# Prompt attention: VectorE's compressed step split around one copy, and the mask conversions placed in the compression stage

## What is computed

```python
s_c = jnp.einsum('bqghd,bngd->bghqn', qg, kc).astype(jnp.float32)
p_c = masked_softmax(s_c, m_c)
o_c = jnp.einsum('bghqn,bngd->bqghd', p_c.astype(vc.dtype), vc)
...
s_s = jnp.einsum('bqghd,bgqkd->bghqk', qg, ks).astype(jnp.float32)
p_s = masked_softmax(s_s, m_s)
o_s = jnp.einsum('bghqk,bgqkd->bqghd', p_s.astype(vs.dtype), vs)
...
s_w = jnp.einsum('bqghd,bkgd->bghqk', qg, k_win).astype(jnp.float32)
p_w = masked_softmax(s_w, m_w)
o_w = jnp.einsum('bghqk,bkgd->bqghd', p_w.astype(v_win.dtype), v_win)
...
o = g[..., 0:1] * o_c + g[..., 1:2] * o_s + g[..., 2:3] * o_w
```

## Time and profile before

| | |
|---|---|
| median of 3 runs | 4078.23 us (4076.43 to 4082.27) |
| the profiled execution | 4081.6 us, its span 4080.0 us, mean granted TensorE clock 0.973 |
| busy over the span | PE 93%, DVE 44%, ACT 23%, POOL 30% |
| prompt attention | from 2443.0 to 2991.3 us of the span |
| in 2500 to 2600 us | PE 93.11, DVE 60.67, ACT 58.77, POOL 60.18 us busy |

### The profile page before, as it was taken

One profiled execution on the slowest core, in us unless ns is written; L12 is line 12 of the kernel. 1 busy time (PEld: TensorE's weight loads), 2 busy tenths in 40 slices (PEclk: granted clock), 3 DMA queues, 4 the chain that ended last, 5 costly groups with the idle time before them and its releaser, 6 DMA issues. The chain is left out here.

```text
span 4080.0 us, 54787 instructions
## 1 busy us (share of the span) xinstructions
PE 3813.7 (93%) x20290; PEld 2936.2 (72%) x20290; DVE 1812.0 (44%) x3004; ACT 941.9 (23%) x2132; POOL 1215.9 (30%) x1021
## 2 busy tenths in 40 slices
PE   8999989998799999999999988999979999999999
PEld 5666666666576888878877766666657688888887
DVE  4565456654443111126662216666645411112766
ACT  3333332333210000000000005656531000000001
POOL 0211112111132333324341105656533233332432
PEclk9999999999699999999999999999989999999999
DMA  4010101100041111123331220000033111111322
GB/s 147 29 40 26 37 27 42 37 26 27 32 125 65 41 41 41 41 82 104 90 124 34 71 76 30 1 2 1 1 94 93 65 41 41 41 41 48 123 86 80
DMA packets 321874, 223.99 MB, mean 55 GB/s; under 512 B 28427, under 2 KB 313220, under 8 KB 319812
## 3 DMA queue, kind: packets, MB, share of 16 engines
q1 hardware_dynamic: 316020, 214.98, 17.7%
q0 software_dynamic: 2048, 5.25, 0.4%
q10 hardware_dynamic: 3650, 1.64, 0.2%
HBM read 191.54 MB, written 34.37 MB: 55 GB/s over the span
## 5 line engine op out<-in xcount | busy, mean ns | idle before, releaser
L773 PE MATMUL ps<-xT,work 128*128 128x272 f32 x2688 | 643.4, 392 | 0.0
L773 PEld LDWEIGHTS ps<-xT,work 128*128 128x128 f32 x2688 | 510.7, 190 | 105.3
L1269 PE MATMUL ps<-xn,work 128*128 128x363 f32 (+1 forms) x1536 | 548.6, 476 | 6.6 <-issue 6.5
L773 PE MATMUL ps<-xn,work 128*128 128x272 f32 x2016 | 489.9, 392 | 3.9 <-DVE work L844 3.9
L773 PEld LDWEIGHTS ps<-xn,work 128*128 128x128 f32 x2016 | 382.9, 190 | 83.9 <-issue 5.1
L387 PE MATMUL ps<-work 128*128 128x272 f32 x1676 | 402.4, 396 | 12.0 <-PEq L741 4.3
L387 PEld LDWEIGHTS ps<-work 128*128 128x128 f32 x1676 | 319.5, 191 | 83.5 <-issue 16.0
L2919 POOL TENSOR_SCALAR work<-work 128x640 f32<-128x640 f32 (+4 forms) x192 | 313.7, 1644 | 196.7 <-DVE work L2822 196.3
L1269 PEld LDWEIGHTS ps<-xn,work 128*128 128x128 f32 x1536 | 261.2, 192 | 102.8 <-issue 18.6
L646 POOL TENSOR_TENSOR xT<-xT,work 128x272 f32<-128x272 f32 x96 | 198.3, 2079 | 263.9 <-DVE work L512 167.1
L1963 POOL TENSOR_TENSOR xT<-xT,consts 128x512 f32<-128x512 f32 x96 | 133.6, 1405 | 453.7 <-DVEq L1793 386.2
(11 more groups left out here) (425 smaller groups left out, 5865.1 us busy)
## 6 DMA issues: line engine op xcount, KB each, us to landing
work<-in_ffn_w_in_dram SPq DMA_DIRECT2D x88, 512.0 KB, 4.9
xn<-in_ffn_w_out_dram SPq DMA_DIRECT2D x46, 704.0 KB, 4.5
work<-in_gdn_w_in_dram SPq DMA_DIRECT2D x32, 512.0 KB, 4.2
work<-in_ffn_w_out_dram SPq DMA_DIRECT2D x18, 704.0 KB, 4.5
ffn_parked_residual<-xT SPq DMA_DIRECT2D x2, 4352.0 KB, 12.8
work<-in_gdn_w_out_dram SPq DMA_DIRECT2D x32, 256.0 KB, 2.8
work<-in_nsa_w_out_dram SPq DMA_DIRECT2D x64, 128.0 KB, 2.9
xT<-ffn_parked_residual SPq DMA_DIRECT2D x4, 1632.0 KB, 10.2
```

The costliest lines, as they stand in the source:

```text
L773: ins = pe.matmul(acc(a, n), w[:, k, :], t[:, k, a * SUB:(a + 1) * SUB], start=(first and k == 0), stop=(k == HK - 1), skip_group_check=True)
L1269: mm = pe.matmul(unit_acc(u, m), w[j % 2][:, k, :], c.xn[:, k, o:o + cnt], start=(k == 0), stop=(k == KD - 1))
```

## The change

There are three edits. In `compress_stage` DVE now makes the bf16 masks and the memset between `keep_bias(0)` and `keep_pairs(1)`; the attention's own conversions, the semaphore and PE's wait for it are gone. `low_masks` only gives both stages the same addresses. In DVE's loop `maxima(k)` takes a list of groups. At the 7 c steps inside the list, g = 0 is done first, then `coefficients(k-1)` and `keep(k-3)`, and then g = 1. In the iteration behind a c step (where k - 1 is the c step), `keep(k-3)` comes before `coefficients(k-1)` and no longer after it.

```diff
@@ compress_stage, vector @@
                 keep_pairs(0)
                 keep_bias(0)
+                ident_low, causal_low, far_low, cmp_low = low_masks(a)
+                dve.tensor_copy(ident_low, const(c, "ident"))
+                dve.tensor_copy(causal_low, const(c, "causal_add"))
+                dve.tensor_copy(far_low, const(c, "far_add"))
+                for x in range(2):
+                    o, _ = CONST[f"cmp_add{4 * x}"]
+                    dve.tensor_copy(cmp_low[x], c.ct[:, o:o + 4 * NCMP])
+                dve.memset(a.rows[:, 0:NC, 4 * P:5 * P].rearrange("p i (g n) -> p i g n", g=2)[:, :, :, NCMP:DH], 0.0)
                 keep_pairs(1)
...
+def low_masks(a):
+
+    low = [a.rows[:, n, 2 * P:3 * P].bitcast(mybir.dt.bfloat16) for n in range(4)]
+    return low[0][:, 0:P], low[0][:, P:2 * P], low[1][:, 0:P], [low[2 + x][:, 0:4 * NCMP] for x in range(2)]
...
@@ prompt_attention, tensor @@
-                pe.wait_ge(low_ready, 1)
                 for k in range(NK + 4):
                     if k < NK:
                         scores(k)
@@ prompt_attention, vector @@
-                def maxima(k):
+                def maxima(k, gs):
                     t, kind, i = steps[k]
-                    for g in range(2):
+                    for g in gs:
                         dve.wait_ge(sc[g], k + 1)
...
-                dve.tensor_copy(ident_low, const(c, "ident"))
-                dve.tensor_copy(causal_low, const(c, "causal_add"))
-                dve.tensor_copy(far_low, const(c, "far_add"))
-                for x in range(2):
-                    o, _ = CONST[f"cmp_add{4 * x}"]
-                    dve.tensor_copy(cmp_low[x], c.ct[:, o:o + 4 * NCMP])
-                dve.memset(pc[:, :, :].rearrange("p i (g n) -> p i g n", g=2)[:, :, :, NCMP:DH], 0.0).then_inc(low_ready, 1)
+                def compressed(k):
+                    return 0 < k < NK and steps[k][1] == "c"
+
                 for k in range(NK + 3):
                     if k < NK:
-                        maxima(k)
+                        maxima(k, (0,) if compressed(k) else (0, 1))
+                    if compressed(k - 1):
+                        keep(k - 3)
                     if 1 <= k <= NK:
                         coefficients(k - 1)
-                    if 3 <= k:
+                    if 3 <= k and not compressed(k - 1):
                         keep(k - 3)
+                    if compressed(k):
+                        maxima(k, (1,))
```

More of the change, by code:

```diff
@@ L2572, in prompt_attention @@
     QT = TP // P
-    BF16 = mybir.dt.bfloat16
     steps = [(0, "c", None)]
@@ L2585, in prompt_attention @@
     pts = [dead[:, n * 512:(n + 1) * 512] for n in range(RING)]
-    low = [a.rows[:, n, 2 * P:3 * P].bitcast(BF16) for n in range(4)]
-    ident_low, causal_low, far_low = low[0][:, 0:P], low[0][:, P:2 * P], low[1][:, 0:P]
-    cmp_low = [low[2 + x][:, 0:4 * NCMP] for x in range(2)]
+    ident_low, causal_low, far_low, cmp_low = low_masks(a)
     probs = {"s": [[take(c, TP) for g in range(2)] for _ in range(2)], "w": [[take(c, 5 * P) for g in range(2)] for _ in range(2)]}
@@ L2658, in prompt_attention @@
     with ExitStack() as ctx:
-        low_ready, sc0, sc1, mx0, mx1, ex0, ex1, cst, cf, scaled, wscaled, tr, kv, ka, multiplied, od = sems(
-            nc, ctx, c, "masks_ready", "scores0_done", "scores1_done", "maxima0_ready", "maxima1_ready", "probs0_ready", "probs1_ready",
+        sc0, sc1, mx0, mx1, ex0, ex1, cst, cf, scaled, wscaled, tr, kv, ka, multiplied, od = sems(
+            nc, ctx, c, "scores0_done", "scores1_done", "maxima0_ready", "maxima1_ready", "probs0_ready", "probs1_ready",
             "chain", "coefficients", "probs_scaled", "window_probs1_scaled", "group_turned", "group_kept_vector", "group_kept_scalar",
```

## The result

The changed kernel is slower: 4090.45 us median (4087.42 to 4094.59, 13 runs) against 4079.90 us (4076.43 to 4083.22, 13 runs) of the kernel before on the same chips. The ratio is 1.0024, with a 95% interval of 1.0018 to 1.0031, so it lost between 7.3 and 12.6 us. I had forecast +4.5 us and a range that ended at 4088 us. The direction was right, the size was less than half of what was measured, and 4090.45 us lies above the range. Part of that is the base: my 4083 us stood on the median of 3 runs, 4078.23 us, and the 13 runs give 4079.90.

A forecast was written before the change was run, and what follows sets the result against it. PE, busy 93% of the span, was taken as the bound. Terms 6.1 + 0 + 0 - 0.95 - 0.8 + 0.15 = +4.5 us on a median of 4078.23 us gave 4082.7, said as 4083 us; range 4077 to 4088 us.

The forecast's parts named there:

- Step 1: At the seven inner c steps: copy 1.31 us earlier, PE's products 0.87 us later, all lost, +6.1 us.
- The distances named as the sign of this: Between c steps: 67.3 us at full clock and 68.8 with a low stretch would confirm that nothing is absorbed.
- Step 2: DVE's iteration behind a c step: copy ahead of the coefficients leaves the instruction order unchanged, 0 us.
- Step 3: PE's clock behind the c steps: 0 us in the sum, from -3.0 to +3.0 us in the range.
- Rival B: Longer gap lowers PE's clock behind every c step, perhaps with a second low stretch; 4086.5 us, chance 18%.
- Step 4: The masks: -0.95 us and -0.8 us at the attention's start, +0.15 us in the compression stage.
- the third term: Masks in the compression stage: idle time covers all but 0.15 us of the six instructions, +0.15 us.
- Rival A: At the c steps only the copy mattered, output early enough; 18.3 us faster with masks and clock, 4060 us, chance 5%.

The follow-up runs named there:

- x5: The changed kernel with 18 useless mask products on PE in the wait at each inner c step; 4078.23 us against 4080.21 us of the kernel before, ratio 0.9996.
- x1: The kernel before with only the masks moved to the compression stage, DVE's loop the old one; 4081.54 us against 4081.05 us, ratio 0.9999.
- x3: The changed kernel with ACT's output(k-4) ahead of both exponentials at the seven inner c steps; 4071.92 us against 4081.05 us of the kernel before, ratio 0.9979.
- x6: The kernel before with 10 useless mask products on PE in its wait at each inner c step; 4073.61 us against 4080.21 us, ratio 0.9981.
- x2: The kernel before with only DVE's loop changed, masks left at the attention's start; 4091.27 us against 4081.05 us, ratio 1.0026.
- x7: x3 with DVE making the c step's coefficients one iteration later, behind maxima(k+2); 4079.56 us against 4080.21 us of the kernel before, ratio 0.9998.
- x4: The kernel before with ACT's output(k-4) ahead of the exponentials at the inner c steps, DVE's order old; 4080.38 us against 4081.05 us, ratio 1.0001.
- x9: x1 with ACT doing output(k-4) and the copy of s(1) ahead of the inner c steps' exponentials; 4068.81 us against 4081.52 us of the kernel before, ratio 0.9969.
- x10: x9 with ACT's copy of w(1) also ahead of the exponentials of w(2); 4067.37 us against 4081.52 us of the kernel before, ratio 0.9968.

## Why the prediction was right and wrong

**Step 1, the split: right.** Copy 1.31 us earlier (measured 1.32), the second pair and the output 0.87 us later (0.87), the products later by 0.87 (0.86), PE's wait from 1.8 to 2.66 us with the output as its releaser, seven times, nothing left for the copy. "I take the whole 0.87 us as lost" was nearly so: x5 shows 0.77 us for each c step, so 5.4 us instead of 6.1, just below the lower bound of 7 x 0.80. The distances named as the sign of this, 67.3 us at full clock and 68.8 with a low stretch, came as 67.23 (x5) and 68.7 to 68.8.

**Step 2, the copy ahead of the coefficients: right.** DVE's stream there is the same.

**Step 3, PE's clock: this is the term that failed.** I had put 0 us into the sum, and +3.0 us as its upper end for "all seven times". The end was set by the count of low stretches and left out their length. A wait of 2.67 us was followed by the low level in seven of seven places in the changed kernel, and in two of them it lasted twice as long, at 2.7 to 2.8 us each. Over the six distances, with x5's 67.23 us as the base at full clock, the clock took 415.1 - 6 x 67.23 = 11.7 us after and 404.8 - 6 x 66.46 = 6.0 us before: +5.7 us where the sum had 0. With 6 x 0.77 = 4.6 us from step 1 that is the 10.3 us found; behind the seventh c step the clock adds 0.1 us. The equal gap had been followed by the low level five times and not twice, which was a reason to expect more from a gap half as long again, so that +3 was likelier than the middle of the range. Rival B named it, "perhaps with a second low stretch", but had no price for that stretch; it is the case that came true, with 18% on it. x5 confirms the cause by taking the idle time away and leaving the delay.

**Step 4, the masks: both terms came, and half of them was given back.** PE's first products of the attention, after:

```profile
2442.35 0.59 PE L2706 MATMUL ps<-work 128*128 128x252 bf16 x4 [2.17 <-PEq L2413]
...
2442.87 2.00 PE L2712 MATMUL ps<-work 64*128 64x63 f32 x32
```

Counted from L2537, PE begins 57.14 us behind it against 58.09, which is the 0.95 us forecast, and the 32 products take 2.00 us instead of 2.83, which is the 0.8. DVE's first reduce is 1.79 us earlier. But from there to the first c step inside the list it takes 16.98 us instead of 16.02, so only 0.83 us are left of 1.6 (0.80 in x1). That the raw times differ by just 1.6 us is chance: the changed kernel's trace was 0.76 us ahead before the change began. No run shows what took the 0.96 us.

In the compression stage the third term failed: L2524 starts 1.13 us behind the first bias copy (2385.21 to 2386.34), as before (2385.97 to 2387.10), so the cost was 0 and not 0.15 us:

```profile
2385.21 0.35 DVE L2537 COPY work<-ps 128x1 f32<-128x1 f32 x4 [34.92 <-PE ps L2481]
...
2386.34 0.07 DVE L2550 MEMSET work<- 128x16 f32 x1
2386.34 2.02 DVE L2524 COPY work<-ps 128x512 f32<-128x512 f32 x2
```

By the runs this gain stays below what x1 could resolve.

Together: +5.4 from the output, +5.8 from the clock and -0.8 from the masks make the 10.3 us found within 0.1, where I had +6.1, 0 and -1.6.

**Rival A's price was wrong too.** It gave 18.3 us if the copy alone had mattered. x3 made that case real and gave 9. Seven waits of 1.31 us were counted as time, though PE and DVE arrived together one step later (where I had read it for the delay but not for the gain): a place with no slack against a delay has none to give to a gain either. x6 gets 6.6 us out of the kernel before with PE's wait filled by useless products.

**Open:** why the first and the fifth low stretch were the long ones. The seven waits are equal to 0.01 us, and x2, with the same waits, has one long stretch, behind its fourth c step. No run here tells what sets it. Nor does the length of the wait alone tell whether a low stretch comes: seven waits of 1.68 us at another place (x7) had none behind them, and waits of 1.8 us at the c steps had one in 16 of 21 places. No run puts a wait of 1.7 us at the c steps or one of 1.8 us elsewhere, and no kernel was profiled twice.

## What to carry to other kernels

Before a wait is shortened, list everything that its end depends on and when each was ready; where the second was ready only 0.05 us before the last, moving the last alone gives nothing, and a move that pushes the second back is a loss. Follow every instruction that a reordering delays through the in-order queues of the other engines, since here a later reduce on VectorE made an exponential on ScalarE later, and with it the unrelated output behind it, for which TensorE waited. And a short idle time of TensorE can be harmless by itself and still cost more than its length in lower clock behind it: look at what the clock did behind each such gap, and price a longer one by the worst row and not by the mean.

## What was not expected of the hardware

- A wait of 1.8 us on TensorE was followed by the lower clock level (1.2 GHz) in five of seven equal places, at 1.5 us each, in six of seven in x1 and five of seven in x4; one of 2.67 us in seven of seven, at 1.5 to 2.8 us each, and again in seven of seven in x2. Waits of 0.5 to 1.2 us in x3, x9 and x10, and seven of 1.68 us in x7, were followed by it nowhere in the stretch of the c steps.
- 18 products of no use in such a wait made the kernel 11 to 12 us faster than without them, and 10 of them made the kernel before 6.6 us faster (x5, x6). The fillers took 0.12 us each (2.11 / 18 and 1.25 / 10).
- DVE's five small conversions and the memset at the head of its copies cost no time at all, where 0.15 us had been worked out: the first of them starts at 2385.49, 0.07 us before the four bias copies have ended (2385.56), and the long copy starts with the memset, which takes 0.07 us.
